# A down projection computed as seven half-size products, with weight sums made by adding DMAs

## The reference

```
h = rms_norm(x, norm_ffn)
x = x + (silu(h @ w_gate) * (h @ w_up)) @ w_down
```

## Time and profile before

| | |
|---|---|
| median of three runs | 1574.59 us |
| span of the profiled execution, first to last instruction | 1570.6 us |
| its own time | not listed apart; the median is 4.0 us above the span |
| PE busy | 1536.9 us (98%) |
| VectorE busy | 1007.2 us (64%) |
| ScalarE busy | 832.5 us (53%) |
| GpSimd busy | 210.5 us (13%) |
| HBM traffic over the span | 149 GB/s |

### The profile page before, as it was taken

The page is one execution under the profiler, slowest core; times in us unless marked ns, Lnnn a source line. Parts: engine busy times, 40 slices in busy tenths (PEclk is TensorE's granted clock), DMA queues, the critical chain, the costliest instruction groups (busy, mean ns, idle before and its releaser), DMA issues.

```text
span 1570.6 us, 20022 instructions
## 1 busy us (share of the span) xinstructions
PE 1536.9 (98%) x7872; PEld 1247.3 (79%) x7872; DVE 1007.2 (64%) x1681; ACT 832.5 (53%) x1459; POOL 210.5 (13%) x278
## 2 busy tenths in 40 slices
PE   9999999999999999999989999999999999999999
PEld 8877777788877888888877766888778888888887
DVE  4267977865479998999787786575765333434231
ACT  5278776554456888888863434435434333333220
POOL 1000014522234000000062101111201000000000
PEclk9999999999999999999999999999999999999999
DMA  6122121114547999999943111031212323223232
GB/s 233 65 81 79 56 71 65 54 54 150 214 161 231 375 421 421 421 422 421 326 149 107 54 54 54 28 108 54 81 58 78 108 81 108 92 82 121 67 112 90
DMA packets 78641, 235.89 MB, mean 150 GB/s; under 512 B 6960, under 2 KB 9424, under 8 KB 66256
## 3 DMA queue, kind: packets, MB, share of 16 engines
q1 hardware_dynamic: 68288, 207.62, 36.3%
q10 hardware_dynamic: 6624, 14.88, 2.5%
q0 software_dynamic: 3632, 12.08, 2.0%
HBM read 221.97 MB, written 12.60 MB: 149 GB/s over the span
## 4 chain that ended last, share of the span: by engine, by line
PE 84%; DVE 11%; ACT 2%; issue 1%; DMA 1%; POOL 0%; SPq 0%; DVEq 0%; ACTq 0%; POOLq 0%
PE bank L109 80%; PE bank L112 4%; DVE low L134 2%; DVE REST L124 1%; DVE REST L134 1%; DVE REST L137 1%; ACT REST L115 1%; DVE AL L124 1%; DVE REST L146 1%; DVE REST L143 1%; DVE REST L130 1%; ACT REST L118 1%; ACT CHH L118 0%; DVE R L124 0%; DVE st L140 0%
## 5 line engine op out<-in xcount | busy, mean ns | idle before, releaser
L124 DVE TENSOR_TENSOR low<-slot,CHH 128x1024 fp32r<-128x1024 f32 (+1 forms) x300 | 298.0, 1037 | 117.5 <-ACT CHH L118 116.5
L118 ACT ACTIVATE CHH<-slot 128x1024 fp32r<-128x1024 f32 (+1 forms) x300 | 258.8, 900 | 128.7 <-PE bank L109 56.6
L134 DVE SCALAR_TENSOR_TENSOR low<-slot,smalls,CHH 128x512 fp32r<-128x512 f32 (+1 forms) x232 | 170.3, 766 | 191.2 <-ACT CHH L118 187.3
L109 PE MATMUL bank<-AH,CHH 128*128 128x512 f32 (+1 forms) x640 | 248.5, 388 | 0.2 <-DVE AL L124 0.2
L109 PE MATMUL bank<-AL,CHH 128*128 128x512 f32 (+1 forms) x640 | 242.8, 379 | 0.0
L109 PE MATMUL bank<-AH,low 128*128 128x512 f32 (+1 forms) x640 | 242.6, 379 | 0.0
L118 ACT ACTIVATE CHH<-slot,smalls 128x512 fp32r<-128x512 f32 (+1 forms) x232 | 154.6, 701 | 137.8 <-PE bank L109 68.2
L109 PE MATMUL bank<-CHH,AH 128*128 128x512 f32 x512 | 215.2, 420 | 3.8 <-DVE low L134 2.8
L109 PE MATMUL bank<-low,AH 128*128 128x512 f32 x512 | 200.8, 392 | 0.0
L109 PE MATMUL bank<-CHH,AL 128*128 128x512 f32 x512 | 200.2, 391 | 0.0
L109 PE MATMUL bank<-CHH,XTF 128*128 128x512 f32 x512 | 161.2, 396 | 1.9 <-DVE REST L121 1.1
(11 more groups left out here) (191 smaller groups left out, 2395.4 us busy)
## 6 DMA issues: line engine op xcount, KB each, us to landing
slot<-in_w_in SPq DMA_DIRECT2D x35, 1024.0 KB, 5.1
slot<-in_w_exp_gate SPq DMA_DIRECT2D x32, 1024.0 KB, 13.0
slot<-in_w_exp_up SPq DMA_DIRECT2D x32, 1024.0 KB, 13.2
slot<-in_w_exp_down SPq DMA_DIRECT2D x32, 1024.0 KB, 13.2
slot<-in_w_gate SPq DMA_DIRECT2D x10, 1024.0 KB, 4.9
slot<-in_w_up SPq DMA_DIRECT2D x10, 1024.0 KB, 5.0
slot<-in_w_down SPq DMA_DIRECT2D x10, 1024.0 KB, 5.1
slot<-in_w_out SPq DMA_DIRECT2D x8, 1024.0 KB, 5.1
```

The lines of the kernel that those rows point to most:

```text
L109: return self.e.matmul(out, l, r, start=start, stop=stop) if self.e else Issued()
L118: return self.e.activation(out, in_, ACT.Copy, scale=scale) if self.e else Issued()
L124: return self.e.tensor_tensor(out, a, b, op) if self.e else Issued()
L134: return self.e.scalar_tensor_tensor(out=out, in0=a, scalar=s, in1=b, op0=op0, op1=op1) if self.e else Issued()
```

## The change

`a` and B are cut in quarters: A11 and A21 are hidden tiles 0 to 10 for tokens 0 to 255 and 256 to 511, A12 and A22 the same for tiles 11 to 21; B11, B12 are rows of tiles 0 to 10 for output columns 0 to 511 and 512 to 1023, B21, B22 those of tiles 11 to 21. The eight quarter products become seven (Winograd's form of Strassen's scheme, with signs turned so that all sums of weights are additions):

- sums of activations, on POOL, on 128x256 tiles: S3 = A11 - A21, S1 = A21 - A22, S2 = S1 - A11, S4 = A12 + S2;
- sums of weights: T3 = B12 + B22 by a DMA that adds B22 from HBM onto the loaded B12; T2 = T3 + B11 and T4 = T2 + B21 on DVE; T1 = B11 + B12 by an adding DMA;
- PE: P1 = A11 B11, then P2 = A12 B21, then for each of the 11 hidden tiles three products together, P6 (S2 T2, added in P1's banks), P7 (S3 T3) and P4 (A22 T4), a **triple**; then P3 (S4 B22, the sixth), and P5 (S1 T1, the seventh, again in P1's banks). A product has 11 chunks x 2 token tiles x 3 passes;
- DVE adds the banks to `xr` in 16 steps (`add_on`) instead of 8.

B11, B12, B21 and B22 are now read several times: nine quarters instead of four. Two slots are new, 9 and 10, at addresses that the layer no longer needs. A triple has one slot of three chunks, filled by two SP loads (512 and 256 KB) and one adding DMA of 256 KB on POOL's queue; eleven triples turn through slots 9, 10, 1, 2, 0.

```diff
 ...
+    def dma_add(self, out, in_):
+        return self.e.dma_start(out, in_, accum_op=ALU.add) if self.e else Issued()
 ...
-    for n in range(2):
-        plan_seg(f"wd{n}", t["w_down_2"][0], 512 * n, 0, nk=FT, part=3)
+    plan_block(0, 0)
+    plan_block(1, 0)
+    in_turn = itertools.cycle((9, 10, next(in_turn), next(in_turn), next(in_turn)))
+    triples = []
+    for j in range(FK):
+        s = plan_slot(next(in_turn), down_rows[:, 0, j, :].rearrange("p (b n) -> p b n", b=2), 3, 512, 3)
+        s.rest = down_rows[:, 1, j, 0:512]
+        s.more = down_rows[:, 1, j, 512:1024]
 ...
+        unit(s, 0, 3, 3 * (j % 2), ("T4", j))
+    pair_cells = itertools.cycle((6, 8, 3, 0))
+    plan_block(1, 512)
+    plan_block(0, 0, add_row=512)
 ...
+        def product(name, c, part, k, two, first, last):
+            hi, lo = high(c), low(c)
+            pe.wait_ge(*at(("part", part, k if part == A11 else k // 3)))
+            pe.wait_ge(*at(("", "lo", c)))
+            for i in range(2):
+                l = [x[:, k, i * P:(i + 1) * P] for x in (part_high[part], parts_low[:, part])]
+                pe.matmul_on(two[i], l[0], hi, first, False)
+                pe.matmul_on(two[i], l[1], hi, False, False)
+                m = pe.matmul_on(two[i], l[0], lo, False, last)
 ...
+        for k in range(FK):
+            c = D0 + 2 * FK + 3 * k
+            product("P6", c, S2, k, sums, False, k == FK - 1)
+            product("P7", c + 1, S3, k, own7, k == 0, k == FK - 1)
+            product("P4", c + 2, A22, k, own4, k == 0, k == FK - 1)
 ...
+        def unit_high(chunks, raws, lows, highs, before, ready):
+            act.wait_ge(*at(ready) if ready else landed(chunks[0]))
+            for c in before:
+                act.wait_ge(*at(("", "done", c)))
+            act.copy(highs, raws).then_inc(*mark("act_hi", *(("", "hi", c) for c in chunks)))
 ...
+        def first_low(k):
+            dve.wait_ge(*at(("S2", k)))
+            dve.wait_ge(*at(("part high", A11, k)))
 ...
+                if FK + 2 <= f < FT - 1:
+                    first_low(f - FK - 2)
 ...
+        def weight_sums(j):
+            b11, b12, b21 = (triples[j].ap[:, q, :] for q in range(3))
+            dve.wait_ge(*at(("added", triples[j].number)))
+            dve.tt(b11, b12, b11, ALU.add).then_inc(*mark("dve_down", ("T2", j)))
+            dve.wait_ge(*at(("T2", j)))
+            dve.tt(b21, b11, b21, ALU.add).then_inc(*mark("dve_down", ("T4", j)))
 ...
+        for u, unit in enumerate(units):
+            if 11 <= u < 11 + FK:
+                weight_sums(u - 11)
+            if u >= len(EARLY_UNITS):
+                unit_low(*unit)
 ...
+        add_on("P5", 1, 1, bank="P1", done=True)
+        add_on("P5", 0, 1, bank="P1", done=True)
 ...
+        for f in range(FT):
+            k = f % FK
+            pool.wait_ge(*at(("a", f)))
 ...
+                pool.tt(parts[:, S1, k, :], parts[:, A21, k, :], parts[:, A22, k, :], ALU.subtract).then_inc(*mark("pool_down", ("S1", k)))
+                pool.wait_ge(*at(("S1", k)))
+                pool.tt(parts[:, S2, k, :], parts[:, S1, k, :], parts[:, A11, k, :], ALU.subtract).then_inc(*mark("pool_down", ("S2", k)))
 ...
+        def add_weights(s, to):
+            pool.wait_ge(sem(f"w_land{s.i}"), s.landed)
+            pool.dma_add(to, s.more).then_inc(*mark(f"w_add{s.i}", ("added", s.number), by=16))
+
+        for s in triples:
+            add_weights(s, s.ap[:, 1, :])
+        for s in sums_last:
+            add_weights(s, s.ap)
 ...
```

More of the change, by code:

```diff
@@ L25 @@
 FT = 22
+FK = 11
+FH = 256
 EPS = 1e-6
@@ L57 @@
 FFN_TURN = 11, 15, 27, 33
+EARLY_UNITS = 8, 10, 12
 class Issued:
@@ L750, in _build, with piece @@
     ss4, r4 = stat(NT), stat(NT)
-    aT = [x[:, :].rearrange("p (f n) -> p f n", f=FT) for x in (AFH, AFL)]
+    parts = AR[:, :].rearrange("p (o k n) -> p o k n", o=7, k=FK)
+    parts_low = AO[:, :].rearrange("p (o k n) -> p o k n", o=7, k=FK)
+    A11, A21, A12, A22, S2, S3, S4 = range(7)
+    S1 = A21
+    part_high = dict(zip((A11, A12, S3, S2, S1), (x[:, :].rearrange("p (k n) -> p k n", k=FK) for x in (HA[0], HA[2], HA[3], HA[1], HA[4]))))
+    part_high[A22], part_high[S4] = part_high[A11], part_high[A12]
+    def piece(x, n):
+        return x[:, 3 * n:min(3 * n + 3, FK), :]
     sgp = ring(split(R1[:, 0:16 * KB], 8), [("sg", f) for f in range(FT)])
@@ L2983, in vector @@
+                if FK + 2 <= f < FT - 1:
+                    first_low(f - FK - 2)
             if f0:
                 drain(seg(f"fg{f0}"))
[L2985 to L2993, removed]
+            for n, _ in enumerate(seg(f"fu{f0}", up_evac)):
+                if f0 == 20 and n in EARLY_UNITS:
+                    unit_low(*units[EARLY_UNITS.index(n)])
@@ new lines, in vector, with add_on @@
+        last_on = {(i, n): ("x4", i, n) for i in range(NT) for n in range(2)}
+        def add_on(name, half, n, bank=None, left=False, done=False):
+            for i in range(2):
+                to = 2 * half + i, n
+                xs = xr[:, to[0], n * 512:(n + 1) * 512]
+                dve.wait_ge(*at(("full", name, i)))
+                dve.wait_ge(*at(last_on[to]))
+                last_on[to] = ("on x", name, *to)
+                events = [last_on[to]]
+                if left:
+                    events.append(("free", (name, i)))
+                if done:
+                    events.append(("out", *to))
+                b = banks.ap((bank or name, i))
+                dve.tt(xs, *((xs, b, ALU.subtract) if n and name != "P3" else (b, xs, ALU.add))).then_inc(*mark("dve_evac", *events))
@@ new lines, in vector @@
+        for u, unit in enumerate(units):
+            if 11 <= u < 11 + FK:
+                weight_sums(u - 11)
+            if u >= len(EARLY_UNITS):
+                unit_low(*unit)
+            if u == 1:
+                first_low(FK - 3)
+            if u == 2:
+                first_low(FK - 2)
+                first_low(FK - 1)
+            if 3 <= u <= 4:
+                for n in (2 * u - 6, 2 * u - 5):
+                    low_of(A12, n)
+            if 5 <= u <= 6:
+                for n in (2 * u - 10, 2 * u - 9):
+                    low_of(S2, n)
+            if 7 <= u <= 8:
+                for n in (2 * u - 14, 2 * u - 13):
+                    low_of(S3, n)
+            if u == 9:
+                add_on("P1", 0, 0)
+            if 10 <= u <= 11:
+                for n in (2 * u - 20, 2 * u - 19):
+                    low_of(A22, n)
+            if u == 14:
+                add_on("P2", 0, 0, left=True, done=True)
+            if 15 <= u <= 18:
+                low_of(S4, u - 15)
+            if 19 <= u <= 22:
+                low_of(S1, u - 19)
+            if u == 25:
+                add_on("P6", 1, 0, bank="P1")
+            if u == 27:
+                add_on("P7", 1, 0)
+                add_on("P4", 1, 0, done=True)
+            if u == 28:
+                add_on("P7", 1, 1)
+            if u == 31:
+                add_on("P3", 0, 1)
@@ L3256, in sync @@
                 sp.dma_start(lamb, t["diff_lambda_2"].to_broadcast([P, 256])).then_inc(*mark("d_lam", "lamb", by=16))
-        for n in range(2):
-            for i in range(NT):
+        for n, half in ((0, 0), (0, 1), (1, 1), (1, 0)):
+            for i in range(2 * half, 2 * half + 2):
                 sp.wait_ge(*at(("out", i, n)))
```

149 lines of the change are left out of this document (127 added, 22 removed).

## The result

The changed kernel took 1577.85 us (median of 7 runs, 1577.10 to 1583.41); the kernel before, on the same chip, 1574.02 (7 runs, 1573.19 to 1575.96). The ratio is 1.0029, 95% interval 1.0018 to 1.0040: slower by 0.3%. The forecast was 1565.9, its range 1562 to 1576, with 0.14 for slower. The profiled execution is the one of 1577.85 us; its span is 1576.0, 1.85 us less. In every execution of the kernel before that was timed beside an experiment, time and span differ by 2.25 to 2.45 us; so some 1.6 of the 4.0 us between its median and the span of its profile mean only that a quick execution was profiled.

A forecast was written before the change was run, and what follows sets the result against it. PE was taken to bound the kernel, so fewer matmuls in the down projection shorten it one for one. -15.0 + 3.2 + 1.7 + 1.4 = -8.7 us, from 1574.6 to 1565.9; range 1562 to 1576.

The forecast's parts named there:

- Matmuls, -15.0: Down projection: 462 matmuls instead of 528, 66 fewer at 0.2267 us each, save 15.0 us.
- VectorE ahead of the first triple, +3.2: P1 and P2: PE is through at 29.9 us, VectorE's low half at 33.1, so PE stands 3.2 us.
- The list of 28.1 us: VectorE's work from the end of its wait for POOL to the first triple's low half, priced at 28.1 us.
- tile 21 is evacuated at about 0.75: Start of P1: VectorE evacuates the hidden tile 21 about 0.75 us after PE's start, then waits for POOL until about 4.5.
- one PE wait of about 3 us: Sign in the changed profile: PE waits about 3 us for a VectorE low half some 30 us into the down projection.
- I price a wait at its length: PE waits in the down projection cost only their length; waits up to 2.3 us had not lowered the clock.
- What an adding DMA takes, 4.75: Triples: an adding DMA of 256 KB takes a = 4.75 us, costing two turns of 0.85, +1.7 us.
- its own formula: Triples: each of two turns costs a - 3.9 where positive; a beyond 5.0 also delays the first triple.
- the slow rival: Triples: adding DMAs taking 8.8 us or more make the kernel slower by over 0.2%; chance 0.14.
- They stay free up to about 15 us each: P5: T1's adding DMAs of 1 MB start 10 us or more ahead and cost nothing up to about 15 us each.
- The end, +1.4: After the last matmul: VectorE adds two banks twice, four sums following in 2.48 us, +1.4 us.
- the forecast's own case: Triples: adding DMAs of 256 KB take a from 3.9 to 6.7 us, time 1564 to 1571; chance 0.55.

The follow-up runs named there:

- the last kernel: All four sums of weights (T1 to T4) formed in DRAM, VectorE's list cut, unit 2 converted later, against the kernel before: 1561.63 us, ratio 0.9917.
- the kernel of all edits together: The change with T1 summed by VectorE, B12 loaded alone, VectorE's list reordered and unit 2 converted later: 1572.39 us, ratio 0.9986 to the kernel before.

## Why the prediction was wrong

- **Matmuls, -15.0: right.** 462 are left, 0.2267 us each where PE runs; the last kernel shows the whole gain when nothing stands in its way.
- **VectorE ahead of the first triple, +3.2: the mechanism right, the size 5.9, and its consequence missed.** The list of 28.1 us was well priced: from 1456.36, when POOL let VectorE go, to the end of the first triple's low half at 1484.85 are 28.5. The start was wrong: "tile 21 is evacuated at about 0.75" left out the early unit that stands ahead of it on VectorE and waits for its load. Converting that unit later gave back 1.5 of the 2.7 us; the other 1.2 were not taken apart. The sign "one PE wait of about 3 us" came true (2.89) partly by luck: PE came to it 2.9 us later than the 29.9 counted, by stops in P1 and P2 that the forecast did not have.
- **"I price a wait at its length": wrong, 1.7 us.** Behind the 2.89 us wait nine matmuls took 3.72 us, with most starts 0.43 apart, about the lower of the clock's two levels (1.2 GHz); the window's granted clock is 0.66. The 2.3 us wait of the earlier trace rows was no bound for one of 2.9. Nor can the row of digits in the earlier trace rows show such a fall: a digit stands for some 39 us, and the changed kernel's page has forty nines too.
- **What an adding DMA takes, 4.75: measured 5.6, with the loop at +6.4 instead of +1.7.** This term decided. By its own formula 5.6 gives two turns of 1.7 and 0.6 at the first triple, some 4. The rest is that I let only the adding DMA be long: it also holds the engines 2.2 times as long as a copy, and the loads beside it stretched too. The second load of a triple lands after 4.8 us in the median beside adding DMAs, 4.1 beside plain ones and 3.9 beside none. In the second turn it took 6.54, against the 5.0 counted for both loads; it was issued almost together with the slowest adding DMA of the triples (7.4 us), and a 1 MB load of B22 came beside it. Which of these two stretched it is not shown. The range for a was argued by bytes ("reads and rewrites as many bytes in all") from a gather; engine time was the scarce thing. The rule of the Trainium skill that stood with the slow rival (Collectives: The Full Stack, The bandwidth ceiling) was the better guide, with 2.2 measured for its factor of two, in engine time. The other (DMA: Bandwidth & Descriptors, Anatomy of one DMA), 2.6 us for 256 KB by my estimate, is contradicted even by the plain copies of that queue, 4.4 beside loads.
- **"They stay free up to about 15 us each": wrong, +3.2.** T1's adding DMAs of 1 MB took 10.0 and 15.5 us, beside stores to `out` that took 13.5 in the median. The one that P5 waited for was issued 14.6 us before PE stopped (1543.49 and 1558.1), took 15.5, and its high and low halves came on top: the cover was counted against the transfer alone.
- **The end, +1.4: right**, 1.5.
- **The rivals.** No single one came true as priced: a of 5.6 lies in the forecast's own case, and the time of the slow one came from four terms that were each short. "If P5 waits" and "the adds take 7 us or more" were named as what would make the forecast wrong. P5 did wait; of the triples' adds one of eleven was that slow, T1's, of three and four times the size, all were.

## What to carry to other kernels

An adding DMA is not a transfer of its bytes: count it as engine time, here 2.2 times a copy, and allow for the loads beside it. Where its operands are known early, put it where the engines idle, in DRAM if need be; the sums that lost 9.7 us beside the triples and P5 cost nothing that could be seen during gate and up, where all four sums cost 0.8 us. And follow a serial list from its first wait: a term that starts "from PE's start" is only as good as what stands ahead of it on that engine.

## What the runs showed of the hardware that was not expected

- Accumulating DMAs into SBUF from HBM: 27.8% of the 16 engines' time for 5.77 MB against 12.5% as plain copies from the same queue.
- VectorE beside POOL, both on SBUF operands: 5.08 us for a pair that takes 1.81 alone.
- The clock. Nine matmuls at the lower level followed a 2.89 us wait; the 2.84 us wait in P5 of the same execution (1561.38) was followed by none, and in the kernel of all edits together a wait of 1.88 us was:

```profile
1524.61 0.50 PE L115 MATMUL bank<-CHH,HA 128*128 128x512 f32 x1 [1.88 <-DVE low L133]
...
1525.78 0.63 PE L115 MATMUL bank<-CHH,AO 128*128 128x512 f32 x1
1526.21 0.63 PE L115 MATMUL bank<-low,HA 128*128 128x512 f32 x1
```

At the same triple of the change a wait of 1.89 us (1524.28) was followed by none. Over all profiles of the experiments and the change, PE waited 2.9 us at the first triple in seven, and each time the lower level followed; of five waits of 2.74 to 2.87 us in P5 two were followed by it. So the length of the last wait alone does not decide; what does was not tried.
